# Hybrid attention and scan block on one core: rounded weights in eight buffers, low parts written over the loaded chunks, conversion five chunks ahead

## The chip, the cores and the metric

The kernel runs on one core of a Trainium2 chip. The metric is the device time of one execution, in microseconds (us). TensorE multiplies matrices, VectorE and ScalarE work on tiles in SBUF and PSUM, GpSimd does a little set-up work, and SyncE issues most of the DMAs. Each engine runs its own list of instructions in order, and semaphores are all that holds one engine back for another.

## The reference, cut to what matters

One layer for 256 tokens of width 2048, all in float32:

```python
h = rms_norm(x, norm_mix_g)
u = h @ w_in                       # 2048 x 12352: q|k|v, z, x|B|C, dt
attn = dilated_window_attention(...)    # 16 heads of 128, three patterns merged
y = ssd_chunked(x, dt, A, B, C)         # 32 heads of 64, 8 groups, both directions
ssd = grouped rms_norm((y_fwd + y_bwd + x * d_skip) * silu(z))
x = x + concat(attn, ssd) @ w_out       # 4096 x 2048
x = x + relu(rms_norm(x) @ w_up)**2 @ w_down    # 2048 x 8192, 8192 x 2048
```

## The kernel before, in words

**Units and chunks.** All large products stream their weights. The stream is cut into 64 units of 512 columns by 2048 rows, and each unit into eight chunks (`CH`), 256 rows by 512 columns, 512 KB. Chunk j of unit U has the number 8U + j; there are 512 of them. Units 0 to 23 are `w_in`, eight windows of three units (`WIN` = 24 chunks or slots), units 24 to 31 are `w_out`, and units 32 to 63 are the MLP, four quarters of four `w_up` units and four `w_down` units.

**Three products for one.** Float32 weights are split into a rounded part of type fp32r and the rest, `w = w_hi + w_lo`, and the activations likewise. TensorE computes hi times lo, lo times hi and hi times hi for every tile (L1154 `chunk_by_weights`, L1170 `chunk_by_tokens`).

**The stations of a chunk.** SyncE loads it into `raw[j]` (L284 `load`); the loads of the scan's x, B and C columns have three pieces. ScalarE rounds it into `w_hi` (L460 `high`). VectorE subtracts into `w_lo` (L767 `low`) and raises `lo_dve`. TensorE waits for `lo_dve` (L274 `wait_low`), multiplies, and raises `chunk_used` by one. There are eight `raw` buffers, and four each (`RING`) of `w_hi` and `w_lo`.

```python
            def load(U, j, pieces):
                if positive(U):
                    wait_low(sp, U - 1, j)
...
                act.wait_ge(raw_in[j], 48 * (U + 1))
                if positive(CH * U + j - RING + 1):
                    act.wait_ge(chunk_used, CH * U + j - RING + 1)
```

So a load waits until VectorE has converted the chunk that the buffer held, and ScalarE waits until TensorE has used the chunk four numbers back.

**Slots.** In every window each engine has a list by slots s = 0 to 23, written out by hand. TensorE multiplies chunk s and then does the slot's other work. ScalarE and VectorE first convert chunk s + `LEAD` (3), by `high_ahead` (L467) and `low_ahead` (L772), and then do the slot's other work. In the MLP the two convert chunk by chunk with no lead written into the list, and only the semaphores limit how far ahead they get. At the end of each MLP quarter VectorE adds up the last result (L1121 `down_add`), which waits for the quarter's last chunk, before it converts the next quarter's first.

**The scan.** The scan's groups G = 0 to 7 are worked on in windows 1 to 4, two to a window, from slot 0 and from slot 12 on (`GROUP_SLOT`). Within a group, k is the slot counted from there. VectorE masks C times B at k = 1 (`mask_cb`, L811), prepares one head at each k = 1 to 4 (`mix_head`, L778, ending with L788), convolves the next group's columns at k = 0, 5, 6, 8, 9 (L790), gates at k = 7 (L818), and normalises at k = 10 and 11. TensorE multiplies C and B at k = 0, the first two heads at k = 4 (once heads 0 and 1 are prepared, two calls of `mix_head` in), the other two at k = 6, and sums the squares at k = 9, for which it needs VectorE's `sq_lo` (L878). ScalarE computes the next group's decay arguments at k = 5, 6, 8, 9 (`decay_args`, L486, six instructions a head), squares the gate at k = 7 (L523), and works through two table loads at k = 10. The decay rows that `decay_args` reads are loaded by SyncE (L315 `load_decay`, two DMAs of 512 KB), and this stands in SyncE's list behind the chunk load of slot 11 or slot 23 (L320), for use in ScalarE's slots 5 and 17. SyncE's list is eight chunks ahead in numbers: the load of slot 11 fills the buffer of slot 3's chunk, and that of slot 23 the buffer of slot 15's.

**Attention and the rest.** Attention heads are worked on four to a window in windows 5 to 7 and beside `w_out`. Their bias tiles are loaded behind the chunk loads of slots 10, 14, 18 and 22 (L331). The residual input `xres`, two DMAs of 1 MB, is loaded behind slot 12's load of the `w_out` units (L372). In the first window ScalarE issues one DMA of 3 MB, `rel_tiles` (L604), and the stores of the decay rows (L609), at slots 8 and 12.

Of the kernel before, what the change touches and what calls it, by code (L numbers as in the profile page):

```python
# [28 lines left out]
P = 128  # L29
# [9 lines left out]
UNIT = 512  # L39
KT = 16  # L40
CH = 8
KC = KT // CH
RING = 4
X_SPLIT = 1280
WIN = 3 * CH
LEAD = 3
COL_Q, COL_K, COL_V, COL_Z, COL_X = 0, 2048, 4096, 6144, 8192
COL_B, COL_C, COL_DT = 10240, 11264, 12288
GROUP_SLOT = (0, 12)
# [28 lines left out]
def build(nc, x, norm_mix_g, w_in, q_norm_g, k_norm_g, rel_bias, conv_w, conv_b, dt_bias, a_log,  # L78
          d_skip, ssd_norm_g, w_out, norm_mlp_g, w_up, w_down, bias_table, out):
    f32, f32r = mybir.dt.float32, mybir.dt.float32r  # L80
    ALU, ACT, AX = mybir.AluOpType, mybir.ActivationFunctionType, mybir.AxisListType
# [14 lines left out]
    with ctx:  # L96
# [4 lines left out]
        top = [end - 4 * words]  # L101

        def place(name, shape, dt=f32, at=None):
            size = 4 * int(np.prod(shape[1:]))
            offset = top[0] if at is None else at
            if at is None:
                top[0] += (size + 31) // 32 * 32
                assert top[0] <= end, (name, top[0], end)
            return nc.alloc_sbuf_tensor_at(name, shape, dt, offset=offset)
# [7 lines left out]
        cat_lo = place("cat_lo", [P, 2 * KT, SEQ], f32r)  # L117
        hid_hi = place("hid_hi", [P, KT, SEQ], f32r, at=cat_base)
        hid_lo = place("hid_lo", [P, KT, SEQ], f32r, at=cat_base + KT * SEQ * 4)
        raw = [place(f"raw{j}", [P, KC, UNIT]) for j in range(CH)]  # L120
        w_hi = [place(f"w_hi{j}", [P, KC, UNIT], f32r) for j in range(RING)]
        w_lo = [place(f"w_lo{j}", [P, KC, UNIT], f32r) for j in range(RING)]
        ident = place("ident", [P, P])
        ones = place("ones", [P, P])
        ones_r = place("ones_r", [P, P], f32r)
# [95 lines left out]
        def bank_pair(n):  # L221
            return psum[:, 2 * n:2 * n + 2, :]

        def tiles(n):

            return bank_pair(n).rearrange("p b (t s) -> p (b t) s", t=2)

        def sem(name):
            return ctx.enter_context(nc.semaphore(name))

        raw_in = [sem(f"raw_in{j}") for j in range(CH)]
        hi_ready, lo_dve, chunk_used = sem("hi_ready"), sem("lo_dve"), sem("chunk_used")
# [37 lines left out]
        def positive(count):  # L270

            return not isinstance(count, int) or count > 0

        def wait_low(eng, U, j):  # L274
            eng.wait_ge(lo_dve, CH * U + j + 1)
# [7 lines left out]
        def _(sp):  # L283
            def load(U, j, pieces):  # L284
                if positive(U):
                    wait_low(sp, U - 1, j)
                at = 0
                for src in pieces:
                    n = src.shape[-1]
                    sp.dma_start(raw[j][:, :, at:at + n], src).then_inc(raw_in[j], 16 * len_of[len(pieces)])  # L290
                    at += n
# [6 lines left out]
            def ssd_window(w, m):  # L298

                for s in range(WIN):  # L300
                    r, j = divmod(s, CH)
                    if r < 2:
                        g = 2 * w + r
                        load(3 * w + r, j, [in_cols(j, COL_X + 256 * g, 256), in_cols(j, COL_B + 128 * g, 128),
                                            in_cols(j, COL_C + 128 * g, 128)])
                        if m is None and s == 5:
                            sp.dma_start(dt_raw[:, :, :], w_in_v[:, :, COL_DT:COL_DT + 64]).then_inc(dtw_in, 16)
                            sp.dma_start(dtcol[:, 0:1], dt_bias[0].rearrange("d (h o) -> (d h) o", o=1)).then_inc(col_in, 16)
                            sp.dma_start(dtcol[:, 1:2], a_log[0].rearrange("d (h o) -> (d h) o", o=1)).then_inc(col_in, 16)
                            sp.dma_start(dskip_all[:, :], d_skip[0:1, :].broadcast_to([P, SSM_HEADS])).then_inc(dskip_in, 16)  # L310
                    else:
                        load(3 * w + r, j, [in_cols(j, COL_Z + UNIT * w)])
                    decay_loads(s, w, m)
# [25 lines left out]
            def att_window(a, m, g):  # L339

                for s in range(WIN):
                    r, j = divmod(s, CH)
                    load(12 + 3 * a + r, j, [in_cols(j, (COL_Q, COL_K, COL_V)[r] + UNIT * a)])
                    if m is not None:
                        decay_loads(s, None, m)
                    if g is not None:
                        load_bias(s, g)
# [89 lines left out]
        def _(act):  # L437
# [16 lines left out]
            def x_high(R):  # L454

                r = R % 8
                act.wait_ge(xg_ready, R + 1)
                act.activation(actT_hi[:, KC * r:KC * r + KC, :], xg[R % 2][:, :, :], ACT.Copy).then_inc(xh_ready, 1)

            def high(U, j):  # L460

                act.wait_ge(raw_in[j], 48 * (U + 1))
                if positive(CH * U + j - RING + 1):
                    act.wait_ge(chunk_used, CH * U + j - RING + 1)
                act.activation(w_hi[j % RING][:, :, :], raw[j][:, :, :], ACT.Copy).then_inc(hi_ready, 1)  # L465

            def high_ahead(U0, s):  # L467

                n, j = divmod(s + LEAD, CH)
                high(U0 + n, j)  # L470
# [121 lines left out]
            act.activation(dtcol[:, 2:3], dtcol[:, 1:2], ACT.Exp).then_inc(dt_act, 1)  # L592
            for s in range(CH - LEAD, WIN):
                high_ahead(0, s)
# [81 lines left out]
            x_high(15)  # L676
            high(MLP_U, LEAD)
            for t in range(TT):
# [16 lines left out]
            def mlp_quarter(q, start):  # L695
                for s in range(start, 8 * CH):
                    n, j = divmod(s, CH)
                    high(MLP_U + 8 * q + n, j)
                    if 1 <= n <= 4 and j == 2:
                        relu(MLP_U + 8 * q + n - 1, n - 1, q)  # L700
                    if 1 <= n <= 4 and j == 3:
                        hid_high(n - 1, q)

            mlp_quarter(0, LEAD + 1)
            with act.Fori(1, 4) as q:
# [4 lines left out]
        def _(dve):  # L710
            tt_, ts_, stt_ = dve.tensor_tensor, dve.tensor_scalar, dve.scalar_tensor_tensor
# [53 lines left out]
                    actT_hi[:, KC * r:KC * r + KC, :].bitcast(f32), ALU.subtract).then_inc(xl_ready, 1)  # L765

            def low(U, j):  # L767
                i = j % RING
                dve.wait_ge(hi_ready, CH * U + j + 1)
                tt_(w_lo[i][:, :, :], raw[j][:, :, :], w_hi[i][:, :, :].bitcast(f32), ALU.subtract).then_inc(lo_dve, 1)  # L770

            def low_ahead(U0, s):  # L772

                n, j = divmod(s + LEAD, CH)
                low(U0 + n, j)
# [254 lines left out]

            for s in range(CH - LEAD, WIN):
                low_ahead(0, s)
# [115 lines left out]
        def _(pe):  # L1148
            def mm(o, lhsT, rhs, first, last, **kw):
                return pe.matmul(o, lhsT, rhs, start=first, stop=last, **kw)  # L1150
# [3 lines left out]
            def chunk_by_weights(U, j, pair):  # L1154


                wait_low(pe, U, j)
                i = j % RING
                res = tiles(pair)
                for kk in range(KC):  # L1160
                    k = KC * j + kk
                    for c in range(4):
                        cols = slice(P * c, P * c + P)
                        for n, (w, a) in enumerate(((w_hi, actT_lo), (w_lo, actT_hi), (w_hi, actT_hi))):
                            ins = mm(res[:, c, :], w[i][:, kk, cols], a[:, k, :],
                                     k == 0 and n == 0 and c % 2 == 0,
                                     k == KT - 1 and n == 2, skip_group_check=True)
                ins.then_inc(chunk_used, 1)

            def chunk_by_tokens(U, j, pair, hi, lo, k0):  # L1170


                wait_low(pe, U, j)
                i = j % RING
                for kk in range(KC):
                    k = KC * j + kk
                    for t in range(TT):
                        toks = slice(P * t, P * t + P)
                        for n, (a, w) in enumerate(((lo, w_hi), (hi, w_lo), (hi, w_hi))):
                            ins = mm(bank_pair(pair)[:, t, :], a[:, k0 + k, toks], w[i][:, kk, :],  # L1180
                                     k == 0 and n == 0, k == KT - 1 and n == 2)
                ins.then_inc(chunk_used, 1)

# [104 lines left out]
            for R in range(3):  # L1288
# [4 lines left out]
                if R == 0:  # L1293
                    pe.wait_ge(consts, 2)
                    pe.wait_ge(rs_diagonal, 2)
                    for t in range(TT):
                        ins = mm(bank_pair(2)[:, 0, P * t:P * (t + 1)], ones[:, :], rs_diag[:, t, :], True, True)
# [10 lines left out]
            for s in range(WIN):  # L1308
                r, j = divmod(s, CH)
# [11 lines left out]
                if s == 13:  # L1321
                    pe.wait_ge(rel_copied, 1)
                    pe.wait_ge(dt_step, DT_STEPS)
                    for i in range(5):
                        ins = pe.transpose(M1[:, 64 * i:64 * i + 64], dt_rows[:, i, :], ident[0:64, 0:64])
# [34 lines left out]
            for n in range(8):  # L1360
                pair = (0, 1, 2, 0, 1, 2, 0, 1)[n]
# [76 lines left out]
```

## Time and profile before

| | |
|---|---|
| median of 3 runs | 1597.03 us (1596.88 to 1598.89) |
| the profiled execution, its own time | 1597.19 us |
| its span in the profile | 1595.5 us |
| TensorE busy (PE) | 1538.2 us, 96% |
| weight loads of TensorE (PEld) | 1377.2 us, 86% |
| VectorE busy (DVE) | 979.7 us, 61% |
| ScalarE busy (ACT) | 778.2 us, 49% |
| mean DMA rate | 183 GB/s |
| `w_lo` L770, VectorE | 512 of 1224 ns |
| `w_hi` L465, ScalarE | 512 of 1057 ns |

Times of rows are in us from the start of the span, unless marked ns. PE is TensorE, DVE VectorE, ACT ScalarE, SPq the queue of SyncE's DMA instructions. In a timeline a row is a start, a duration, the engine, the line, the operation and its tiles; brackets at its end hold the idle time of the engine just before and what ended it. The matmuls of the kernel's helper all bear L1150.

### The profile page before, as it was taken

What the parts mean: (1) busy time and instruction counts of PE and PEld (TensorE: products, weight loads), DVE (VectorE), ACT (ScalarE), POOL (GpSimd) and SP (SyncE); (2) the same over time, 40 slices, a digit from 0 to 9 for tenths busy, and PEclk for the clock granted to TensorE, in tenths of its full rate; (3) what the DMA queues carried; (4) which work ended last, traced back from release to release, by engine and by line L of the source; (5) the groups of instructions that cost most, each with busy time, mean ns of one, the idle gap of its engine ahead of it and who ended that gap; (6) DMA issues with size and microseconds to landing.
All of it is one profiled execution on the core that took longest, in us unless ns stands there. A gap on an engine that the chain in (4) does not pass through costs nothing.

```text
span 1595.5 us, 25920 instructions
## 1 busy us (share of the span) xinstructions
PE 1538.2 (96%) x9501; PEld 1377.2 (86%) x9501; DVE 979.7 (61%) x1362; ACT 778.2 (49%) x1075; POOL 24.2 (2%) x29
## 2 busy tenths in 40 slices
PE   6999899888999999999999999999999999999998
PEld 6999888886788888888889998899988998889987
DVE  5787788888876666665466555455554455535553
ACT  4377666666655545444344443334433444334432
POOL 0000000000101010000000000000000000000000
PEclk9999999999999999999999999999999999999999
DMA  9875556555565656565656656656565655656552
GB/s 256 257 222 163 144 157 181 164 168 172 150 195 166 185 174 183 177 236 169 197 185 179 181 181 198 185 172 185 186 197 170 182 183 192 192 167 184 185 195 95
DMA packets 186336, 291.59 MB, mean 183 GB/s; under 512 B 13533, under 2 KB 67151, under 8 KB 185984
## 3 DMA queue, kind: packets, MB, share of 16 engines
q1 hardware_dynamic: 183748, 285.92, 59.1%
q10 hardware_dynamic: 2492, 4.36, 0.9%
q8 instruction: 63, 1.03, 0.3%
q14 instruction: 33, 0.27, 0.1%
HBM read 288.04 MB, written 5.34 MB: 184 GB/s over the span
## 4 chain that ended last, share of the span: by engine, by line
PE 79%; DVE 11%; issue 5%; ACT 3%; DVEq 1%; DMA 0%; ACTq 0%
PE psum L1150 77%; DVE w_lo L770 2%; DVE mix L784 2%; DVE conv L804 2%; ACT w_hi L465 1%; ACT L532 1%; DMA x_in<-in_x 0%; DVE conv L800 0%; DVE cbm L815 0%; ACT conv_t L507 0%; PE psum L1249 0%; PE psum L1269 0%; PE psum L1195 0%; DVE gate_t L822 0%; DVE gate_t L845 0%
## 5 line engine op out<-in xcount | busy, mean ns | idle before, releaser
L770 DVE TENSOR_TENSOR w_lo<-raw,w_hi 128x1024 fp32r<-128x1024 f32 x512 | 625.1, 1224 | 501.7 <-ACT w_hi L465 496.2
L465 ACT ACTIVATE w_hi<-raw 128x1024 fp32r<-128x1024 f32 x512 | 539.7, 1057 | 654.5 <-PE psum L1150 651.4
L1150 PE MATMUL psum<-actT_lo,w_hi 128*128 128x256 f32 x1792 | 516.0, 288 | 16.8 <-DVE w_lo L770 16.8
L1150 PE MATMUL psum<-actT_hi,w_lo 128*128 128x256 f32 x1792 | 511.8, 286 | 0.0
L1150 PE MATMUL psum<-actT_hi,w_hi 128*128 128x256 f32 x1792 | 511.4, 285 | 0.0
L1150 PEld LDWEIGHTS psum<-actT_lo,w_hi 128*128 128x128 f32 x1792 | 348.7, 195 | 26.0 <-DVE w_lo L770 19.1
L1150 PEld LDWEIGHTS psum<-actT_hi,w_lo 128*128 128x128 f32 x1792 | 348.7, 195 | 0.2
L1150 PEld LDWEIGHTS psum<-actT_hi,w_hi 128*128 128x128 f32 x1792 | 348.8, 195 | 0.0
L1150 PE MATMUL psum<-w_hi,hid_lo 128*128 128x512 f32 x512 | 199.2, 389 | 0.0
L1150 PE MATMUL psum<-w_lo,hid_hi 128*128 128x512 f32 x512 | 199.2, 389 | 0.0
L1150 PE MATMUL psum<-w_hi,hid_hi 128*128 128x512 f32 x512 | 199.2, 389 | 0.0
L1150 PE MATMUL psum<-w_hi,actT_lo 128*128 128x512 f32 x384 | 154.1, 401 | 2.8 <-DVE w_lo L770 2.8
L1150 PE MATMUL psum<-w_lo,actT_hi 128*128 128x512 f32 x384 | 150.8, 393 | 0.0
L1150 PE MATMUL psum<-w_hi,actT_hi 128*128 128x512 f32 x384 | 150.5, 392 | 0.0
L1150 PEld LDWEIGHTS psum<-w_hi,hid_lo 128*128 128x128 f32 x512 | 96.1, 188 | 20.0
L1150 PEld LDWEIGHTS psum<-w_hi,hid_hi 128*128 128x128 f32 x512 | 96.1, 188 | 20.0
L1150 PEld LDWEIGHTS psum<-w_lo,hid_hi 128*128 128x128 f32 x512 | 96.1, 188 | 19.6
L1150 PE MATMUL psum<-w_hi,cat_lo 128*128 128x512 f32 x256 | 100.8, 394 | 0.0
L1150 PE MATMUL psum<-w_hi,cat_hi 128*128 128x512 f32 x256 | 99.8, 390 | 0.0
L1150 PE MATMUL psum<-w_lo,cat_hi 128*128 128x512 f32 x256 | 99.8, 390 | 0.0
L1150 PEld LDWEIGHTS psum<-w_hi,actT_lo 128*128 128x128 f32 x384 | 72.5, 189 | 19.3 <-DVE w_lo L770 4.8
L1150 PEld LDWEIGHTS psum<-w_hi,actT_hi 128*128 128x128 f32 x384 | 72.5, 189 | 16.1
(192 smaller groups left out, 1150.7 us busy)
## 6 DMA issues: line engine op xcount, KB each, us to landing
raw<-in_w_in SPq DMA_DIRECT2D x128, 512.0 KB
raw<-in_w_up SPq DMA_DIRECT2D x128, 512.0 KB
raw<-in_w_down SPq DMA_DIRECT2D x128, 512.0 KB
raw<-in_w_out SPq DMA_DIRECT2D x64, 512.0 KB
raw<-in_w_in SPq DMA_DIRECT2D x64, 256.0 KB
raw<-in_w_in SPq DMA_DIRECT2D x128, 128.0 KB
decay<-decay_rows SPq DMA_DIRECT2D x16, 512.0 KB, 5.7
rel_tiles<-rel_rows ACTq DMA_DIRECT2D x1, 3072.0 KB, 18.9
```

The lines of the kernel that those rows point to most:

```text
L465: act.activation(w_hi[j % RING][:, :, :], raw[j][:, :, :], ACT.Copy).then_inc(hi_ready, 1)
L532: act.activation(log_ms[:, :], mean_sq[:, :], ACT.Ln).then_inc(ln_ready, 1)
L770: tt_(w_lo[i][:, :, :], raw[j][:, :, :], w_hi[i][:, :, :].bitcast(f32), ALU.subtract).then_inc(lo_dve, 1)
L784: ins = stt_(w[:, k0:k1, :], w[:, k0:k1, :], tokp[:, src, ds(col, 1)], cbm[:, k0:k1, :], ALU.mult, ALU.mult)
L804: stt_(conv[:, c, :], src, wt, conv[:, c, :], ALU.mult, ALU.add).then_inc(conv_step, 1)
L1150: return pe.matmul(o, lhsT, rhs, start=first, stop=last, **kw)
```

## The change

The low part of a chunk is written over the loaded chunk, so `w_lo[j]` is the same memory as `raw[j]`. The memory of the four `w_lo` buffers goes to `w_hi`, which has eight. The load of a chunk waits for `chunk_used` of the chunk eight numbers back, where it waited for `lo_dve`. ScalarE's wait for `chunk_used` before rounding goes. `LEAD` is 5, where it was 3. The decay arguments are on ScalarE in both kernels; no line of them differs. The edits in `chunk_by_tokens` are those of `chunk_by_weights`.

```diff
-RING = 4
-LEAD = 3
+LEAD = 5
...
+        raw_at = [top[0] + 4 * KC * UNIT * j for j in range(CH)]
         raw = [place(f"raw{j}", [P, KC, UNIT]) for j in range(CH)]
-        w_hi = [place(f"w_hi{j}", [P, KC, UNIT], f32r) for j in range(RING)]
-        w_lo = [place(f"w_lo{j}", [P, KC, UNIT], f32r) for j in range(RING)]
+        w_lo = [place(f"w_lo{j}", [P, KC, UNIT], f32r, at=raw_at[j]) for j in range(CH)]
+        w_hi = [place(f"w_hi{j}", [P, KC, UNIT], f32r) for j in range(CH)]
...
             def load(U, j, pieces):
                 if positive(U):
-                    wait_low(sp, U - 1, j)
+                    sp.wait_ge(chunk_used, CH * (U - 1) + j + 1)
...
                 act.wait_ge(raw_in[j], 48 * (U + 1))
-                if positive(CH * U + j - RING + 1):
-                    act.wait_ge(chunk_used, CH * U + j - RING + 1)
-                act.activation(w_hi[j % RING][:, :, :], raw[j][:, :, :], ACT.Copy).then_inc(hi_ready, 1)
+                act.activation(w_hi[j][:, :, :], raw[j][:, :, :], ACT.Copy).then_inc(hi_ready, 1)
...
             def low(U, j):
-                i = j % RING
                 dve.wait_ge(hi_ready, CH * U + j + 1)
-                tt_(w_lo[i][:, :, :], raw[j][:, :, :], w_hi[i][:, :, :].bitcast(f32), ALU.subtract).then_inc(lo_dve, 1)
+                tt_(w_lo[j][:, :, :], raw[j][:, :, :], w_hi[j][:, :, :].bitcast(f32), ALU.subtract).then_inc(lo_dve, 1)
...
                 wait_low(pe, U, j)
-                i = j % RING
...
-                            ins = mm(res[:, c, :], w[i][:, kk, cols], a[:, k, :],
+                            ins = mm(res[:, c, :], w[j][:, kk, cols], a[:, k, :],
```

## Rows read from the trace of the kernel before

**Rows 1.** The waits of TensorE, 124 to 426 us: us in total, times, longest.

```profile
PE psum L1150 <- DVE mix L788: 16.2, 7, 3.0
PE psum L1150 <- DVE w_lo L770: 10.1, 8, 2.5
PE psum L1150 <- DVE sq_lo L878: 4.1, 3, 1.7
```

**Rows 2.** The waits of VectorE in the same stretch.

```profile
DVE w_lo L770 <- ACT w_hi L465: 36.5, 13, 3.8
```

**Rows 3.** Timeline of VectorE, one group of the scan; start, us, then the idle before.

```profile
240.87 1.15 DVE L815 TENSOR_TENSOR cbm<-psum,mask 128x256 f32<-128x256 f32 x4
...
255.49 1.22 DVE L770 TENSOR_TENSOR w_lo<-raw,w_hi 128x1024 fp32r<-128x1024 f32 x1
...
263.25 1.22 DVE L770 TENSOR_TENSOR w_lo<-raw,w_hi 128x1024 fp32r<-128x1024 f32 x1 [2.31 <-ACT w_hi L465]
...
274.91 1.23 DVE L770 TENSOR_TENSOR w_lo<-raw,w_hi 128x1024 fp32r<-128x1024 f32 x1 [2.93 <-ACT w_hi L465]
...
287.41 1.15 DVE L815 TENSOR_TENSOR cbm<-psum,mask 128x256 f32<-128x256 f32 x4
```

**Rows 4.** Timeline of ScalarE, the same group.

```profile
248.89 1.28 ACT L495 ACTIVATE mix<-decay,tokn 128x128 f32<-128x128 f32 x4 [3.21 <-PE psum L1150]
...
252.79 1.06 ACT L465 ACTIVATE w_hi<-raw 128x1024 fp32r<-128x1024 f32 x1 [2.04 <-PE psum L1150]
...
260.97 0.63 ACT L523 ACTIVATE gate_sq<-gate 128x512 f32<-128x512 f32 x1 [3.50 <-DVE gate L827]
...
262.17 1.04 ACT L465 ACTIVATE w_hi<-raw 128x1024 fp32r<-128x1024 f32 x1
```

**Rows 5.** Timeline of TensorE, the same group.

```profile
247.07 1.70 PE L1150 MATMUL psum<-mix,xtok 128*64 128x256 f32 x8 [2.48 <-DVE mix L788]
```

**Rows 6.** Timeline of TensorE at a turn of the MLP's loop.

```profile
1226.45 0.39 PE L1150 MATMUL psum<-actT_lo,w_hi 128*128 128x256 f32 x1 [2.73 <-DVE w_lo L770]
```

**Rows 7.** Timeline of VectorE, where the scan's first group begins.

```profile
100.94 1.23 DVE L770 TENSOR_TENSOR w_lo<-raw,w_hi 128x1024 fp32r<-128x1024 f32 x1 [1.59 <-ACT w_hi L465]
...
105.64 1.14 DVE L815 TENSOR_TENSOR cbm<-psum,mask 128x256 f32<-128x256 f32 x4
...
120.71 1.23 DVE L770 TENSOR_TENSOR w_lo<-raw,w_hi 128x1024 fp32r<-128x1024 f32 x1 [0.36 <-ACT w_hi L465]
```

**Rows 8.** Timeline of TensorE, the first group's products of C and B.

```profile
102.97 1.03 PE L1150 MATMUL psum<-xbc 128*128 128x256 f32 x4
```

**Rows 9.** Timeline of ScalarE, the first three units and the scan's first group.

```profile
76.87 1.06 ACT L465 ACTIVATE w_hi<-raw 128x1024 fp32r<-128x1024 f32 x1 [1.81 <-PE psum L1150]
...
112.66 1.06 ACT L465 ACTIVATE w_hi<-raw 128x1024 fp32r<-128x1024 f32 x1 [1.82 <-PE psum L1150]
...
116.64 1.28 ACT L495 ACTIVATE mix<-decay,tokn 128x128 f32<-128x128 f32 x4
```

**Rows 10.** SyncE's issues of the chunk loads: ns min/median/max of one.

```profile
L290 SPq DMA_DIRECT2D raw<-in_w_in x320: 367/393/1344, 4.9 to 638.1; - x160
```

**Rows 11.** Timeline of SyncE: one pair of decay loads.

```profile
104.15 0.88 SPq L318 DMA_DIRECT2D decay<-decay_rows  x2
```

**Rows 12.** The tile decay: from issue to landing of its 16 DMAs.

```profile
DMA to landing us min/median/max: 4.2/5.7/7.2
```

**Rows 13.** DMA issues: size of one, median us to landing.

```profile
bias_t<-rel_tiles SPq DMA_DIRECT2D x16, 192.0 KB, 3.7
xres<-in_x SPq DMA_DIRECT2D x2, 1024.0 KB, 9.3
```

**Rows 14.** Vector operations by form: one that writes over its own input.

```profile
L1077 DVE TENSOR_TENSOR xres<-psum,xres 128x1024 f32<-128x1024 f32 x4 | 4.9, 1218 | 0.0
```

**Rows 15.** Stretches: busy us of each engine, TensorE clock, DMA share, GB/s.

```profile
53.00:72.00 19.00, 19.00 (x160) 18.80 (x160) 18.30 (x37) 8.35 (x8) 0.00 (x0) 1.00 0.94 287
...
200.00:300.00 100.00, 89.14 (x674) 84.00 (x673) 82.30 (x157) 63.21 (x119) 0.00 (x0) 0.93 0.59 169
```

More of the change, by code:

```diff
@@ L1173, in chunk_by_tokens @@
                 wait_low(pe, U, j)
-                i = j % RING
                 for kk in range(KC):
@@ L1179, in chunk_by_tokens @@
                         for n, (a, w) in enumerate(((lo, w_hi), (hi, w_lo), (hi, w_hi))):
-                            ins = mm(bank_pair(pair)[:, t, :], a[:, k0 + k, toks], w[i][:, kk, :],
+                            ins = mm(bank_pair(pair)[:, t, :], a[:, k0 + k, toks], w[j][:, kk, :],
                                      k == 0 and n == 0, k == KT - 1 and n == 2)
```

## The prediction

> **What bounds the kernel now.** The table of busy times comes first: TensorE is busy for 96% of the span, some 57 us short of it, so everything the change can give lies in its waits. Those are read next. The stretch from 124 to 426 us, most of the scan, holds 30.4 us: 16.2 us for the prepared heads, 10.1 us for `w_lo`, 4.1 us for `sq_lo` [rows 1]. All three come from VectorE. So the third view is who VectorE waits for, and the reader is to see what is absent there: TensorE. Its large wait is the 36.5 us for ScalarE's `w_hi` [rows 2].
>
> The timelines of one group show what stands behind that. From its masking at 240.87 us to the next group's at 287.41 us VectorE needs 46.5 us for 12 slots, and twice it stops for `w_hi`, for 2.31 and 2.93 us [rows 3]. ScalarE was not held by TensorE before the first of these. It waited 3.50 us for VectorE's own gate, squared it at 260.97, and rounded the next chunk only at 262.17 [rows 4]. This is a closed loop of VectorE and ScalarE: gate, square, round, subtract. ScalarE does wait for TensorE elsewhere (3.21 and 2.04 us, the second on the ring of four) [rows 4], but VectorE takes that chunk only at 255.49 us, 1.6 us after the rounding's end [rows 3]. TensorE is the one that follows: it stands 2.48 us until head 1 is prepared [rows 5]. Outside the scan, three more waits of the kind of 2.73 us lie at the turns of the MLP's loop [rows 6], behind VectorE's `down_add`.
>
> **The change, part by part.**
>
> More lead (3 to 5) and eight `w_hi`. At every slot VectorE and ScalarE keep the same list, one conversion and the slot's work; only the chunk's number grows. The two extra conversions are done in the first window, where VectorE waited for ScalarE, and ScalarE for TensorE, in many slots [rows 7, 9]. The `w_lo` waits (10.1 us) should go. But the first two heads are due at TensorE's k = 4 and prepared in VectorE's k = 2 in both kernels, so TensorE arrives there earlier and stands longer. The sum of the waits is set by VectorE's loop, and nothing in it gets shorter. Worth: 0 in groups 1 to 7.
>
> The start of the loop. Here TensorE did hold VectorE: 1.59 us at 100.94 and 0.36 us at 120.71 through the ring [rows 7]. The masking at 105.64 can't come before TensorE's product of C and B, which ends at 104.0 [rows 8]. So at most 1.6 + 0.4 = 2.0 us can be gained. That is the lower bound of the sum; I take none of it, for the next part.
>
> The later loads. A load now waits until TensorE has used the buffer. For the chunks this is cheap: the buffer of chunk c - 8 is freed seven chunks before TensorE needs c, 20 us at the 2.88 us of a chunk (1.82 idle and 1.06 busy on ScalarE in each) [rows 9]. How long one load alone takes no row shows; 192 KB land in 3.7 us, two of 1024 KB behind other loads in 9.3 us [rows 13]. I take 5, being nearer to the small one, plus 1.2 us for issuing three pieces at 0.39 [rows 10]. ScalarE wants the chunk two uses after the buffer is free, 5.8 us, and it could not start earlier before either. So this costs nothing.
>
> The decay loads are what moves. They stand in SyncE's list behind the chunk load of slots 11 and 23, and are wanted in ScalarE's slots 5 and 17. Before, they went out when VectorE had converted the chunk of slot 3 or 15, so about three chunks earlier. Now they go out when TensorE has used it.
> - First group (arguments of group 1). TensorE ends slot 3's chunk at 112.66 (the rounding that waited for it starts then) [rows 9]. Three pieces, 1.2 us [rows 10], then the pair, whose second issue starts some 0.45 us later [rows 11]: 114.4. Landing takes 4.2, 5.7 or 7.2 us (least, median, most) [rows 12]: 118.6, 120.1 or 121.6, against 116.64 for the arguments before [rows 9]. Behind them come six instructions, 1.85 us at the spacing of 0.31 us, and the rounding of 1.06 us, which VectorE needed by 120.71 [rows 7]. It gets it at 123.0 with the median, 2.3 us later; 0.8 and 3.8 us are the bounds. VectorE has nothing else to do before it, so this moves the whole loop.
> - The group before (arguments of group 0). Slot 15's chunk is used at 76.87 [rows 9]; by the same steps the rows land at 84.3 (median). ScalarE then has, to its slot 23, four sets of arguments (1.85 us), six roundings and two copies of 1 us, some 15 us, and catches up at about 100, so VectorE's masking moves by 0 to 1 us. The later 123.0 is set by the DMA alone and contains it: 0.
> - Groups 1 to 7. In the group shown slot 3's chunk ends at 247.07 - 2.48 - 2.88 = 241.7 [rows 5, 9]; the rows land at 241.7 + 1.7 + 7.2 = 250.6 at the latest. Arguments and rounding end 2.9 us later, at 253.5, and VectorE wants the chunk at 255.49 [rows 3]. Hidden by 2 us, more with the median. What is the cover? TensorE's wait for the heads at k = 4, which is exactly what group 0 lacks. Cost 0.
>
> The bias tiles go out behind slot 10's load and are wanted after the same slot's rounding, so the load's own time covers them. `xres`, 2 MB, now goes out after chunk 196 and delays the load behind it by some 6 us; ScalarE's slot 8 may start some 2 us late there, and TensorE needs its result only in slot 9. Cost 0, with 1 us as the bound above.
>
> Writing `w_lo` over `raw`. The same operation on the same shape, writing over its input, took 1218 ns [rows 14], against 1224 for `w_lo`. Cost 0. Nothing touches `down_add`, so the three waits of rows 6 stay.
>
> TensorE's clock. The short waits merge into longer ones. After the 2.48 us wait eight small matmuls took 1.70 us [rows 5], and over 200 to 300 us the granted clock was 0.93, that is partly at 1.2 GHz [rows 15]. While VectorE sets the end this is free. At the last group's k = 4, TensorE is the bound again afterwards, and one such fall there would cost 1 to 2 us. I take 0 and keep 2 for the range. The Trainium skill (TensorE: Matmul & The Clock Gate, HAM oscillation) says that gaps in TensorE's work let its clock fall again, each time at a cost; by that rule the merged wait would add the upper figure.
>
> **The sum.** 1597.2 + 2.3 = 1599.5 against the profiled execution's own time, which lies 0.2 above the median: 1599.3 against the median. A measurement of this kernel tells 0.2%, 3.2 us, from no change. With the bounds (-2.0 or +0.8 below; +3.8, +1 and +2 above) the case reaches from 1595 to 1604.
>
> **The rivals.**
> - The `w_lo` waits are real time. For it: they are the waits that the change aims at, 10.1 us, and eight of them. Against it: VectorE shows no wait for TensorE between 124 and 426 us. If VectorE had slack that its list hides, 1597.0 - 10.1 = 1587.
> - Slower: the decay rows come late in every group. The place is ScalarE's k = 5. It decides from a landing of 9.3 us on (the 7.2 of the sum and the 2 us of cover); with 11 us each of the seven groups would lose 1.7 us more, 1599.3 + 12 = 1611. For it: the loads now crowd together, as each waits for TensorE. Against it: fewer are in the queue, and 7.2 was the longest of 16 [rows 12]. The Trainium skill (DMA: Bandwidth & Descriptors, Rules for kernel authors) asks for a DMA to be issued early and waited for late; by that rule this change is a step back, and this rival is what it would look like.
> - Slower: the first window. From 53 to 72 us the DMA engines were 94% busy [rows 15], with the 3 MB of `rel_tiles`. Loads issued late meet it there. Were the store of the decay rows, behind slot 12's rounding on ScalarE, 4 us later than I reckon, group 0 would start 4 us late: 1603. The buffers' 20 us speak against TensorE itself starving.
>
> **How the numbers follow.** The closed loop with the late first decay rows: 0.64. In it, below 1593.8 about 0.02, above 1600.2 about 0.21. The `w_lo` rival 0.14. Decays late everywhere 0.09, the first window 0.08. The loop gaining at its start with the decays landing early, 1595: 0.05. Slower is 0.21 + 0.09 + 0.08 = 0.38, faster 0.02 + 0.14 = 0.16, the same 0.46. The range is 1594 to 1605; outside it are the first two rivals, and most else is within.
>
> **What would show it.** In the changed kernel's profile: TensorE's waits for `w_lo` in the scan near nothing, those for the heads grown to some 27 us; the distance of two maskings 44 to 46.5 us as before; a new wait of ScalarE L495 for `decay` at about 116 us, 2 to 5 us long, and none or short ones in later groups; no wait of VectorE for TensorE. I am wrong if the maskings come closer together, if ScalarE's roundings wait for `raw` loads inside the scan, or if VectorE's L770 takes longer than 1.23 us.

## The result and the profile after

The changed kernel takes 1605.32 us (median of 6 runs, 1602.86 to 1607.18) against 1597.13 us; the ratio is 1.0047, with a 95% interval of 1.0036 to 1.0058. The change makes the kernel slower by about half a per cent. The profiled execution took 1605.49 us with a span of 1603.8 us, 8.3 us above the span of before.

The page's head, and then the waits of TensorE and of VectorE from 124 to 440 us (us in total, times, longest), answer to [rows 1, 2]. Lines have moved a little: L768 is `low`, L782 and L786 `mix_head`, L464 `high`, L494 `decay_args`.

```profile
span 1603.8 us, 25424 instructions
...
PE 1542.3 (96%) x9501; PEld 1382.2 (86%) x9501; DVE 972.6 (61%) x1362; ACT 768.6 (48%) x1075; POOL 24.3 (2%) x29
```

```profile
PE psum L1148 <- DVE mix L786: 30.5, 7, 7.0
PE psum L1148 <- DVE sq_lo L876: 3.8, 3, 2.4
```

```profile
DVE w_lo L768 <- ACT w_hi L464: 44.7, 15, 5.2
```

TensorE's waits for `w_lo` in the scan, 10.1 us, are gone. Those for the prepared heads have grown from 16.2 to 30.5 us, that is by more than what went. VectorE still shows no wait for TensorE; it waits for ScalarE's `w_hi`, 44.7 us against 38.8 in the same stretch of the kernel before (the 36.5 of [rows 2] end at 426 us). The 3.01 us at 197.90 below are in the 44.7; experiment 1 shows that they belong to another cause.

The timeline of VectorE in the changed kernel (start, us, and in brackets the idle time before), to be laid beside [rows 3, 7]:

```profile
105.59 1.15 DVE L813 TENSOR_TENSOR cbm<-psum,mask 128x256 f32<-128x256 f32 x4
...
125.66 1.23 DVE L768 TENSOR_TENSOR w_lo<-raw,w_hi 128x1024 fp32r<-128x1024 f32 x1 [5.22 <-ACT w_hi L464]
...
155.34 1.15 DVE L813 TENSOR_TENSOR cbm<-psum,mask 128x256 f32<-128x256 f32 x4
...
197.90 1.23 DVE L768 TENSOR_TENSOR w_lo<-raw,w_hi 128x1024 fp32r<-128x1024 f32 x1 [3.01 <-ACT w_hi L464]
...
202.60 1.15 DVE L813 TENSOR_TENSOR cbm<-psum,mask 128x256 f32<-128x256 f32 x4
...
246.87 1.15 DVE L813 TENSOR_TENSOR cbm<-psum,mask 128x256 f32<-128x256 f32 x4
...
425.59 1.15 DVE L813 TENSOR_TENSOR cbm<-psum,mask 128x256 f32<-128x256 f32 x4
```

The maskings (L813) are the loop's milestones, one to a group. Against the kernel before, the eight of them are later by -0.05, 5.06, 5.75, 6.00, 6.03, 6.27, 6.27 and 6.26 us. So the loss comes in one piece, between the first and the second, with 0.7 us more before the third. It sits in front of the chunk at 125.66 (120.71 before), where VectorE stood 5.22 us for `w_hi`. ScalarE's timeline says why, and SyncE's when it began:

```profile
67.03 1.06 ACT L464 ACTIVATE w_hi<-raw 128x1024 fp32r<-128x1024 f32 x1 [12.91 <-DMA raw<-in_w_in]
...
84.37 1.28 ACT L494 ACTIVATE mix<-decay,tokn 128x128 f32<-128x128 f32 x4 [4.64 <-DMA decay<-decay_rows]
...
111.67 1.06 ACT L464 ACTIVATE w_hi<-raw 128x1024 fp32r<-128x1024 f32 x1 [3.04 <-DMA raw<-in_w_in]
...
122.81 1.28 ACT L494 ACTIVATE mix<-decay,tokn 128x128 f32<-128x128 f32 x4 [6.85 <-DMA decay<-decay_rows]
...
164.82 1.28 ACT L494 ACTIVATE mix<-decay,tokn 128x128 f32<-128x128 f32 x4 [5.56 <-DMA decay<-decay_rows]
...
255.41 1.28 ACT L494 ACTIVATE mix<-decay,tokn 128x128 f32<-128x128 f32 x4 [4.62 <-DMA decay<-decay_rows]
```

```profile
115.19 0.88 SPq L319 DMA_DIRECT2D decay<-decay_rows  x2
```

The decay rows went out from 115.19 us on, and ScalarE, which before began the arguments at 116.64, stood 6.85 us and began at 122.81. The same happens in front of the very first arguments (84.37 against 80.72 before) and in the second and the fourth group (164.82 and 255.41), where VectorE does not feel it. ScalarE also waited for chunk loads in the scan's first group: 1.20, 3.04 and 2.17 us, ending at 107.57, 111.67 and 114.90. Experiment 1 tells whether these cost anything.

The last 2 us lie at the other end of the scan. TensorE's timeline there, and the stretches around it (us, busy us of each engine, TensorE's clock, DMA share, GB/s):

```profile
431.77 1.98 PE L1148 MATMUL psum<-mix,xtok 128*64 128x256 f32 x8 [4.67 <-DVE mix L786]
...
440.70 1.08 PE L1148 MATMUL psum<-mix,xtok 128*64 128x256 f32 x8
```

```profile
426.00:428.00 2.00, 1.10 (x5) 0.56 (x4) 1.90 (x8) 2.00 (x4) 0.00 (x0) 1.00 0.66 236
...
430.00:432.00 2.00, 0.23 (x2) 0.26 (x4) 1.97 (x6) 2.00 (x3) 0.00 (x0) 0.50 0.15 55
...
434.00:436.00 2.00, 2.00 (x6) 1.52 (x6) 1.97 (x5) 0.00 (x0) 0.00 (x0) 0.50 0.01 4
```

The same two products in the kernel before, with the one wait between them and the scan's end:

```profile
425.50 1.08 PE L1150 MATMUL psum<-mix,xtok 128*64 128x256 f32 x8 [0.94 <-DVE mix L788]
...
432.18 1.08 PE L1150 MATMUL psum<-mix,xtok 128*64 128x256 f32 x8
```

After a wait of 4.67 us TensorE's clock is granted at 0.50, the level of 1.2 GHz, and the way from the product at k = 4 to that at k = 6 takes 8.93 us; before, with 0.94 us of wait and the clock at 1.00, it took 6.68. That is 2.25 us. With the 6.26 it makes the 8.5 us by which the second product is late, and the span ends 8.3 us late.

### The profile page after: what moved, and what is told of

The parts are those of the page before. It is cut to its first block, busy times and chain, and to the rows that moved or that the text cites. A ratio compares the mean times of both kernels' runs of the same rounds, so it can differ in the third digit from the quotient of the medians.

```text
span 1603.8 us, 25424 instructions
## 1 busy us (share of the span) xinstructions
PE 1542.3 (96%) x9501; PEld 1382.2 (86%) x9501; DVE 972.6 (61%) x1362; ACT 768.6 (48%) x1075; POOL 24.3 (2%) x29
## 4 chain that ended last, share of the span: by engine, by line
PE 78%; DVE 11%; issue 5%; ACT 4%; DVEq 1%; DMA 1%; ACTq 0%; SPq 0%
PE psum L1148 77%; DVE w_lo L768 2%; DVE mix L782 2%; DVE conv L802 2%; ACT w_hi L464 1%; ACT L531 1%; DMA x_in<-in_x 1%; DVE conv L798 0%; DVE cbm L813 0%; ACT conv_t L506 0%; PE psum L1245 0%; PE psum L1265 0%; DMA decay<-decay_rows 0%; PE psum L1191 0%; DVE gate_t L820 0%
## 5 line engine op out<-in xcount | busy, mean ns | idle before, releaser
L768 DVE TENSOR_TENSOR w_lo<-raw,w_hi 128x1024 fp32r<-128x1024 f32 x512 | 612.4, 1222 | 234.5 <-ACT w_hi L464 229.1
L464 ACT ACTIVATE w_hi<-raw 128x1024 fp32r<-128x1024 f32 x512 | 529.5, 1054 | 416.6 <-DMA raw<-in_w_down 164.8
L1125 DVE SCALAR_TENSOR_TENSOR acc<-psum,inv_ms,acc 128x512 f32<-128x512 f32 x32 | 22.6, 747 | 149.2 <-PE psum L1148 149.2
L1112 DVE TENSOR_TENSOR relu_sq<-relu_t 128x1024 f32<-128x1024 f32 x16 | 19.6, 1225 | 148.9 <-ACT relu_t L688 148.9
```

The lines of the kernel that those rows point to most:

```text
L464: act.activation(w_hi[j][:, :, :], raw[j][:, :, :], ACT.Copy).then_inc(hi_ready, 1)
L768: tt_(w_lo[j][:, :, :], raw[j][:, :, :], w_hi[j][:, :, :].bitcast(f32), ALU.subtract).then_inc(lo_dve, 1)
L1112: tt_(relu_sq[:, :, :], relu_t[:, :, :], relu_t[:, :, :], ALU.mult).then_inc(relu_squared, 1)
L1125: stt_(acc[:, n, t, :], bank_pair(n)[:, t, :], inv_ms[:, 2, t:t + 1], acc[:, n, t, :], ALU.mult, ALU.add).then_inc(down_added, 1)
```

## The experiments

Theory A says that the scan's loop lost its time to the decay rows alone, and that the clock at the last wait did the rest. Theory B says that it was the later chunk loads or the longer lead. A table of what the experiments gave stands first. Medians are of 4 to 11 executions, each ratio is against executions of the kernel before made beside them, and the maskings and the span are from the one profiled execution of each.

| kernel | median us | ratio, 95% interval | 2nd masking | 3rd | last | span |
|---|---|---|---|---|---|---|
| before | 1597 | | 150.28 | 196.85 | 419.33 | 1595.5 |
| changed | 1605.3 | 1.0047 (1.0036 to 1.0058) | 155.34 | 202.60 | 425.59 | 1603.8 |
| 1 changed, decay rows early | 1606.6 | 1.0056 (1.0042 to 1.007) | 150.27 | 199.26 | 424.61 | 1599.2 |
| 2 before, decay rows late | 1612.7 | 1.0094 (1.0079 to 1.011) | 155.72 | 202.30 | 434.96 | 1611.1 |
| 3 changed, lead 3 | 1602.7 | 1.0026 (1.0014 to 1.0039) | 154.75 | 202.38 | 425.44 | 1601.4 |
| 4 changed, leads 5 and 4 | 1579.0 | 0.9879 (0.9863 to 0.9895) | 149.23 | 192.93 | 400.85 | 1578.2 |
| 5 as 4, decay rows early | 1581.1 | 0.9893 (0.9877 to 0.9908) | 146.62 | 192.04 | 403.18 | 1580.6 |
| 6 as 1, windows written out | 1592.1 | 0.9968 (0.9956 to 0.998) | 149.35 | 193.31 | 412.66 | 1589.1 |
| 7 as 4, written out, MLP ahead | 1561.9 | 0.9777 (0.9763 to 0.979) | 149.20 | 190.11 | 394.42 | 1561.1 |
| 8 before, windows written out | 1590.6 | 0.9957 (0.9943 to 0.997) | 149.91 | 193.88 | 413.40 | 1589.4 |
| 9 changed, windows written out | 1597.5 | 0.9998 (0.9989 to 1.0007) | 153.64 | 197.58 | 416.85 | 1593.9 |
| 10 as 7, decay rows early | 1559.3 | 0.976 (0.9747 to 0.9774) | 145.44 | 186.34 | 390.60 | 1557.6 |
| 11 changed, leads 4 and 3 | 1577.2 | 0.9875 (0.9857 to 0.9893) | 147.36 | 190.98 | 399.39 | 1575.3 |

**1. Decay rows three chunks earlier, in the changed kernel.**

```diff
-                if s == 11 and m is not None:
+                if s == 8 and m is not None:
...
-                if s == 23 and w is not None:
+                if w is not None and s == (20 if positive(w) else 23):
```

> The changed kernel with one edit: the decay rows' loads stand behind the chunk loads of slots 8 and 20 instead of 11 and 23, three chunks earlier (the very first pair keeps its place). Theory A (the 6.3 us that the scan's loop lost come from decay rows landing late in the first groups, and 2.2 us more from TensorE's clock falling at the last wait for the heads): ScalarE L494 waits for decay under 2 us in all after the first pair, the second masking returns from 155.3 to about 150.3 us, the maskings after it to those of the kernel before, and the time to 1599, since the merged wait at the last group and its clock stay. Theory B (the chunk loads or the longer lead cost the time, the decay rows only stand beside it): the second masking stays near 155 us and the time near 1605.

The second masking is at 150.27 us, where it was before the change, and ScalarE no longer waits for `decay` at all after the first pair. That part of theory A is shown. The chunk loads are as late here as in the changed kernel, and ScalarE waited 6.6 us for them in the scan (6.4 there), so they cost the loop nothing. But the time did not come back: the third masking is 2.4 us late again. VectorE's timeline at the turn of its window loop:

```profile
188.91 0.88 DVE L851 SCALAR_TENSOR_TENSOR cat_lo<-gate_t,parB,cat_hi 128x256 f32 x2 [1.42 <-ACT cat_hi L537]
194.55 1.23 DVE L768 TENSOR_TENSOR w_lo<-raw,w_hi 128x1024 fp32r<-128x1024 f32 x1 [4.76 <-issue]
...
199.26 1.14 DVE L813 TENSOR_TENSOR cbm<-psum,mask 128x256 f32<-128x256 f32 x4
```

"issue" means that the profile shows nothing it waited for: `w_hi` was rounded long before. In the kernel before the same stand is 2.35 us. In the changed one it is the 3.01 us at 197.90, which the profile puts down to ScalarE's `w_hi`; that chunk had been rounded from 193.65 us on, though, and was long done, so I take it for the turn as well; in experiment 9, where the windows are written out, it is gone. Here the pair of decay rows, 1 MB, was issued at 185.89 us, and VectorE's turn followed at 189.8. The second turn costs 4.72 us against 2.29. The one edit did this, since the changed kernel has 3.01 and 2.34 us at these two turns. It was new, and became theory C: the turn of VectorE's loop is slower with that traffic in the queues. The profiled execution, 1600.9 us, was also the fastest of the five, and the others (1605 to 1607.3) have no profile, so where they lost 5 us more was not seen.

**2. Decay rows three chunks later, in the kernel before.**

```diff
-                if s == 11 and m is not None:
+                if s == 14 and m is not None:
```

> The kernel before with one edit: the decay rows loaded behind slot 11 are loaded behind slot 14, three chunks later; ring of four, lead of three and all chunk loads as before. Theory A: the rows for the second group land at 123 to 124.5 us, VectorE's chunk at 120.7 moves to 126 to 127.5, every later masking is 5 to 7 us later, and the time is 1602 to 1604, without the clock's part, because TensorE's waits for w_lo still split its waits. Theory B: nothing here is on the path, and the time stays at 1597 to 1598.

This delays the rows alone, with the ring, the lead and all chunk loads as they were, and the time is 1612.7 us, 9 us above the upper end of what theory A expected. ScalarE waits for the rows in all four groups that are served from slot 14 (us in total, times, longest):

```profile
ACT mix L495 <- DMA decay<-decay_rows: 36.4, 4, 11.3
```

The second masking moved by 5.4 us, as expected, and three more groups then lost 4.5, 3.5 and 1.9 us; I had expected only the first. Theory B can't explain any of it. Only the first of the four losses stands for the change's own: there the pair goes out at 116.08 us, close to the changed kernel's 115.19, but the later ones go out 11 to 16 us later than in the changed kernel (211.57 us against 200.89, and so on).

**3. Lead 3 with eight buffers.**

```diff
-LEAD = 5
+LEAD = 3
```

> The changed kernel with LEAD 3 instead of 5. Theory A: the decay rows are as late as in the changed kernel, so the second masking stays near 155 us; TensorE waits for w_lo again, which splits the long waits for the heads, and if its clock then does not fall at the last of them the time is 1603, else 1605. Theory B with the lead as the cost: 1597 to 1598. Theory B with the later chunk loads as the cost: 1605 or more.

The second masking is at 154.75 us, 0.6 us ahead of the changed kernel's, and the last at 425.44, level with it (425.59). So the lead isn't what the loop lost. TensorE waits for `w_lo` again, and less for the heads (60 to 470 us: us in total, times, longest):

```profile
PE psum L1148 <- DVE mix L786: 16.4, 7, 3.0
PE psum L1148 <- DVE w_lo L768: 11.4, 7, 3.5
```

Its last wait is 2.54 us instead of 4.67, and from the k = 4 to the k = 6 product it takes 8.30 us, still slow: its clock fell there as well, a little later. The median is 2.6 us below the changed kernel's. The split of the waits does help, but I had expected that the fall would not come at all.

**4. Two leads.**

```diff
-LEAD = 5
+LEAD = 4
+ACT_LEAD = 5
```

with `ACT_LEAD` in place of `LEAD` in ScalarE's list.

> The changed kernel with two leads: ScalarE rounds five chunks ahead, VectorE subtracts four ahead. If VectorE's stops for w_hi in the scan (2.3 and 2.9 to 3.8 us in each group) are only the order of the lists, ScalarE doing its slot's work before the next rounding, they vanish: the distance of two maskings falls from 44 to 46.5 us to about 41, where TensorE's own work sets it, and the time to 1575 to 1585. If the stops are VectorE's own chain (gate, square, tables) and the rounding only stands behind it, the distance stays above 43 us and the time above 1600.

18 us faster than the kernel before. VectorE's timeline at k = 8 and k = 10 to 11, and then the same group in the kernel before, where it stood 2.31 and 3.84 us:

```profile
212.90 1.22 DVE L769 TENSOR_TENSOR w_lo<-raw,w_hi 128x1024 fp32r<-128x1024 f32 x1
214.35 0.69 DVE L877 TENSOR_TENSOR sq_lo<-gate_sq,sq_hi 128x512 fp32r<-128x512 f32 x1 [0.23 <-ACT sq_hi L525]
...
221.65 1.23 DVE L808 SCALAR_TENSOR_TENSOR xbc<-conv_t,conv 128x1024 f32<-128x1024 f32 x1 [0.84 <-ACT conv_t L507]
...
225.12 0.42 DVE L836 SCALAR_TENSOR_TENSOR newton<-rnorm 128x256 f32<-128x256 f32 x1 [1.10 <-ACT rnorm L534]
...
233.14 1.14 DVE L814 TENSOR_TENSOR cbm<-psum,mask 128x256 f32<-128x256 f32 x4
```

```profile
219.24 1.23 DVE L770 TENSOR_TENSOR w_lo<-raw,w_hi 128x1024 fp32r<-128x1024 f32 x1 [2.31 <-ACT w_hi L465]
...
231.81 1.22 DVE L770 TENSOR_TENSOR w_lo<-raw,w_hi 128x1024 fp32r<-128x1024 f32 x1 [3.84 <-ACT w_hi L465]
```

It converts at 212.90 without a stop, because the chunk was rounded a slot earlier, and does so while ScalarE squares the gate; of the 2.31 us 0.23 are left, of the later stop of 3.84 us 0.84 and 1.10. From 192.93 to 233.14 this group takes 40.2 us instead of 44.0; the seven distances are 40.2 to 43.8 us, where they were 43.8 to 46.6. From the first masking to the last the scan is 18.2 us shorter, which is all that the median gained. So the closed loop was real, and most of the idle time in it was only the order of two lists.

**5. Two leads and early decay rows.**

> The kernel with two leads (ScalarE five, VectorE four) and the decay rows three chunks earlier, as in the first experiment. In the kernel with two leads VectorE stops for w_hi only once more, 3.3 us in the first group behind late decay rows. Theory C (a turn of VectorE's loop costs more when the 1 MB of decay rows is in the DMA queues at the same moment, 4.7 instead of 2.3 us): the 3.3 us go, two turns cost 2.4 us more each, and the time is 1577 to 1582, no gain. Without theory C it is 1575 to 1577.

The second masking is 2.6 us earlier, and both turns cost more, 9.7 us together against 4.8 in experiment 4. The net is no gain, as theory C has it.

**6. Early decay rows, and VectorE's windows written out.**

```diff
-            with dve.Fori(1, 4) as w:
+            for w in range(1, 4):
                 ssd_window(w, w - 1)
```

> The first experiment's kernel (decay rows three chunks earlier, lead five for both engines) with VectorE's three scan windows written out instead of a loop; the other engines keep their loops. Theory C: VectorE's two stands of 4.7 us with no releaser before w_lo are its loop's turn, and they go. The distances of all maskings are then 43.8 to 44.7 us, the last one is at about 415 us, and the time is 1593 to 1596, the rest being TensorE's clock at the last wait. If the stands are something else (a late w_hi, TensorE), they stay and the time is 1600 or more.

The stands without a releaser are gone, the distances of the maskings are 43.8 to 44.4 us, and the last is at 412.66. The time, 1592.1 us, is 1 us below the expectation. So the stands were the turns of VectorE's own loop; the other engines' loops are as they were. The last masking is 12.0 us earlier than in experiment 1 and the median 14.5 us lower; where the other 2.5 us went was not taken apart.

**7. Two leads, windows written out, and the MLP's turn.** VectorE converts three chunks of the next quarter before it adds up this one's last result:

```diff
+                for j in range(ahead):
+                    low(MLP_U + 8 * q + 8, j)
                 down_add(MLP_U + 8 * q + 7, 3, q)
...
-            with dve.Fori(1, 4) as q:
-                mlp_quarter(q, 0)
+            with dve.Fori(1, 3) as q:
+                mlp_quarter(q, 3, 3)
+            mlp_quarter(3, 3, 0)
```

> The kernel with two leads, VectorE's scan windows written out, and in the MLP VectorE converting three chunks of the next quarter before it adds the last result of this one. The three waits of 2.7 us at the quarters' turns go, some 8 us, and of the two turns of the scan's loop (2.4 us each) at most 4.8 us: 1566 to 1572, against 1579. If TensorE sets the end of the scan by now, only the MLP's part comes, 1571.

1561.9 us, 4 us more gained than expected. TensorE's waits from 60 us to the end:

```profile
PE psum L1152 <- DVE mix L787: 13.9, 7, 4.2
PE psum L1152 <- issue: 1.0, 2, 0.5
```

There is none for `w_lo` any more. From the last masking to the end of the span it takes 1166.7 us, against 1177.4 in experiment 4: 10.7 us, of which three waits of 2.6 to 2.7 us are 8.1. The rest fits the clock (the section on the hardware): in experiment 4 it was granted at 0.50 for some 6 us behind the first of these waits, and in experiment 7 the MLP has no wait of that kind left to fall behind. It was not measured by itself.

**8. The kernel before, windows written out.**

> The kernel before with VectorE's three scan windows written out, nothing else. If VectorE's and ScalarE's closed loop sets the scan's time, every microsecond taken from it shows: the two stands of 2.3 us go, the last masking comes at about 414.7 instead of 419.3 us, and the time is 1592 to 1593. If TensorE's waits for w_lo were the bound, it stays at 1597.

The last masking is 5.9 us earlier, a little more than the 4.6 us of the two stands, and the span 6.1 us shorter. What is taken from VectorE's loop comes off the end in full, in a kernel where TensorE still waits for `w_lo`; in the scan these waits shrank with it, from 10.1 to 3.7 us. This is also the kernel to lay beside experiment 6, which has the eight buffers, the lead of five and rows in time: its last masking is only 0.7 us earlier (412.66 against 413.40), and its median, 1592.1 against 1590.6 us, is not lower. With the turns and the late rows out of the way the change by itself gains nothing.

**9. The changed kernel, windows written out.**

> The changed kernel with VectorE's three scan windows written out, the decay rows as late as in the change. It is the fourth corner to the kernel before, the first experiment and that one with the windows written out. If the late decay rows and the loop's turns are two separate losses, the second masking stays near 155 us, the distances after it are 43.8 to 44.1 us, the last masking is at about 418.5, and the time is 1597 to 1600: 6 to 8 us above the kernel of early decay rows with the windows written out (1592.1). If the decay rows only mattered through the turns, it comes down to 1592.

1597.5 us, the second masking at 153.64: against experiment 6 the late rows cost 4.3 us at the second masking and 5.4 us in the median, with no turn in sight. The two losses are separate.

**10. Experiment 7 with early decay rows.**

> The fastest kernel so far (two leads, windows written out, MLP's next quarter converted ahead; 1561.9) with the decay rows three chunks earlier. VectorE has no turn in the scan to collide with now, and its one stop behind late decay rows, 3.8 us in the first group, should go. If VectorE still sets the scan's time: 1557 to 1559. If TensorE sets it by now: no change, 1561 to 1562.

1559.3 us, 38 us below the kernel before and the fastest here. The second masking is 3.8 us earlier, and so are the last and nearly the span (3.5 us). The median shows 2.5 of it.

**11. Leads 4 and 3.**

> The changed kernel with ScalarE four chunks ahead and VectorE three, so VectorE's lead is that of the kernel before. If what pays in the two-lead kernel (1579.0) is that ScalarE is one chunk ahead of VectorE, the time is 1577 to 1583. If it is the length of the lead, VectorE's stops for w_hi stay gone but TensorE waits for w_lo again, and the time is 1590 or more.

1577.2 us, as in experiment 4. What pays is the one chunk by which ScalarE is ahead of VectorE, not the length of the lead: experiment 3, with VectorE's lead the same and ScalarE's one shorter, took 1602.7 us.

## Where the prediction was right, and where its sum fell short

**The bound.** That VectorE and ScalarE form a closed loop which TensorE follows was right, and it decided the case. The `w_lo` waits went, the waits for the heads took their place (30.5 us where 27 were forecast), and from the third masking on the distances did not change by more than 0.3 us. Experiments 4 and 8 show the bound from the other side.

**The place and the cause.** The forecast named the arguments of the second group, at VectorE's chunk of 120.71 us. It moved there, to 125.66, and for that reason (experiments 1 and 2, and 9 against 6).

**Its size.** The step that fell short is the term of 2.3 us, with bounds of 0.8 and 3.8; it measured 4.95. It was put together as 114.4 us for the second issue plus the median landing of 5.7 us. Three things were short. TensorE was itself 0.6 us later (its product at k = 4 at 116.00 instead of 115.43). From the start of slot 11's load to the pair SyncE needed 1.83 us (113.36 to 115.19), where 1.2 had been taken for three pieces; in the kernel before it was 1.82 (102.33 to 104.15), so this could have been read. With both the pair began at 115.19, not 114.0. And the two DMAs of the pair landed 5.1 and 6.9 us after issue; ScalarE waits for both. In the kernel before this same pair took 5.2 and 7.2 us. In each of the eight pairs of either kernel one landing is at 5.6 us or less and the other at 5.8 or more, so the median over both members was the wrong row to take. The row's highest value, 7.2, was the one that answered to what ScalarE waits for.

**The clock.** I took 0 and kept 2 us as a bound; it was 2.25 us. The merged wait was foreseen (4.67 us), and once it was, the fall was the likelier case. The Trainium skill (TensorE: Matmul & The Clock Gate, HAM oscillation) says that gaps in TensorE's work make its clock fall, at a cost each time; this trace agrees, with 0.50 granted after the 4.67 us.

**Costed at nothing, and nothing it was.** The later chunk loads: the prediction's own figures, 6.2 us for a load and 5.8 us until it is wanted, already did not fit, and it named waits of ScalarE's roundings for `raw` in the scan as a sign of being wrong. They came, 6.4 us in the first group. They cost nothing all the same, as experiment 1 has them too with its second masking back at 150.27; the sign was a poor one. The first window: ScalarE did wait 12.91 us for a chunk that came in beside `rel_tiles` and began the first arguments at 84.37 (84.3 forecast), yet the first masking was at 105.59 us against 105.64. Later groups: ScalarE waited for decay rows in the second and the fourth group (5.56 and 4.62 us), which are not the short waits that were forecast, and the loop did not feel them. `xres` and the bias tiles: no wait of TensorE between 440 us and the MLP. Writing over `raw`: L768 took 1222 ns on average, 1224 before. The three waits at the MLP's turns stayed.

**Missed.** The turn of VectorE's loop, 0.7 us of the 6.26, was in no term. It stood in the trace of before as 2.35 and 2.29 us without a releaser, and was not read.

**The verdict.** Added up with the measured terms, 4.95 at the chunk, 0.1 behind it, 0.7 at the turn, 0.5 in smaller steps and 2.25 of clock are 8.5 us. The range ended at 1605, and the median of 1605.3 lies on its edge (1605 would be a ratio of 1.0050, measured is 1.0047). The likeliest case, within 0.2%, did not come; slower, at 0.38, did. That the range reached so far is in part luck: it holds 1 us for `xres` that did not come, while the first group's term came out above its own bound of 3.8 us and the turn was in no term. With the pair's landing taken at its long end and the clock's fall as the likelier case, the same working would have given 1603.

## What to carry to other kernels

Deeper buffers help only an engine that is held by buffers. Here TensorE waited for the work of a loop between two other engines, and its waits just changed their name; ask of every wait that you remove what the same engine is due to wait for next. A load that stands in a queue behind another moves with it, so when a queue's wait is changed, every DMA behind it must be given a new time, the last of a group by its longest landing. And where two engines hand each other work in a fixed order, letting the first run one step further ahead than the second can be worth more than the depth of both.

## What the runs showed of the hardware

**The turn of a loop.** At the two turns of its window loop VectorE stands 2.35 and 2.29 us in the kernel before, 3.01 and 2.34 us in the changed kernel, 2.35 and 2.54 in experiment 2, 3.40 and 2.96 in experiment 3, 2.44 and 2.32 in experiment 4, 4.76 and 4.72 in experiment 1, and 4.16 and 5.50 in experiment 5; in the last two, decay rows had been issued up to 4 us before. How busy the DMA engines were during the stand goes with it: a share of 0.01 in the kernel before and in experiment 2, 0.51 to 0.61 where it took 2.3 to 2.4 us, 0.71 to 0.74 where it took 3.0 to 3.4, and 0.82 to 1.01 where it took 4.2 to 5.5. No run varied that load by itself. The first turn in the kernel before and in experiment 1 (DMA share and GB/s are the last two numbers), and what the profile has of instruction queues in the first:

```profile
189.80:192.10 2.30, 1.13 (x10) 0.93 (x8) 0.00 (x1) 2.30 (x6) 0.00 (x0) 1.00 0.01 4
```

```profile
189.80:194.50 4.70, 4.70 (x42) 4.70 (x41) 0.00 (x0) 4.70 (x12) 0.00 (x0) 1.00 0.91 279
```

```profile
q14 instruction: 1, 0.01, 0.9%
```

Writing three windows out took the stands away. The Trainium skill (Runtime: NRT & Kernel Launch, Instruction fetch mechanics) says that a taken branch out of the fetched pages must wait for a DMA. The runs fit that: one packet of the instruction queue q14 falls into each of the fourteen stands named here, and in experiment 8 there is none from 186 to 196 us nor from 275 to 285. The profile does not say for which engine the packet is.

**The clock after a short wait.** TensorE's wait of 2.63 us at the MLP's first turn is the same in every kernel but those of experiments 7 and 10, which have none, but what follows is not. In experiment 1 the clock stayed at 1.00, and the next wait of that kind ended 182.2 us later; in the changed kernel it was granted at 0.50 for about 3 us, and 183.7 us passed. The two stretches, experiment 1 first, then the changed kernel:

```profile
1049.00:1052.00 3.00, 2.59 (x21) 2.59 (x22) 3.00 (x4) 0.96 (x2) 0.00 (x0) 1.00 0.39 142
```

```profile
1051.00:1054.00 3.00, 2.97 (x14) 2.97 (x15) 3.00 (x3) 1.06 (x1) 0.00 (x0) 0.50 0.34 130
```

So this fall cost 1.5 us, and whether one comes after a wait of 2.6 us varies. In the kernel before the clock fell after waits of 2.94 us (203.06) and even 2.12 us (293.61), and not after 3.03 us (381.74). That this makes up the few microseconds by which executions of one kernel differ is possible, but was not tested.
